# Peer-expert v rows: both halves of a row multiplied in turn, and its ring place released with them

## The reference, cut to what matters

```python
def peer(x, w_q, sub_keys, u_tab, v_tab):
    ...
    best, pos = lax.top_k(cand, PEER_TOPK)
    idx = jnp.take_along_axis(cand_idx, pos, axis=-1).reshape(t, PEER_HEADS * PEER_TOPK)
    gate = jax.nn.softmax(best, axis=-1).reshape(t, PEER_HEADS * PEER_TOPK)
    ...
        act = jax.nn.gelu(jnp.einsum('ted,td->te', jnp.take(u_tab, ib, axis=0), xb).astype(f32),
                          approximate=False)
        w = (gb * act).astype(x.dtype)
        return jnp.einsum('te,ted->td', w, jnp.take(v_tab, ib, axis=0))
```

## Time and profile before

| | |
|---|---|
| median of 3 runs | 3233.33 us (3222.72 to 3244.48) |
| span of the profiled execution | 3176.3 us |
| that execution's own time | not given; the median lies 57.0 us above the span |
| mean granted clock of TensorE | 0.81 of full speed |
| busy: TensorE matmul, VectorE, GpSimd, ScalarE | 63%, 56%, 47%, 12% |
| moved by the gathers (GpSimd's queue) | 805 MB of 959 MB |

### The profile page before, as it was taken

One profiled execution on the slowest core, in us unless ns is written; L12 is line 12 of the kernel. 1 busy time (PEld: TensorE's weight loads), 2 busy tenths in 40 slices (PEclk: granted clock), 3 DMA queues, 4 the chain that ended last, 5 costly groups with the idle time before them and its releaser, 6 DMA issues.

```text
span 3176.3 us, 27801 instructions
## 1 busy us (share of the span) xinstructions
PE 2008.3 (63%) x10194; PEld 1164.2 (37%) x10194; DVE 1763.4 (56%) x3957; ACT 378.2 (12%) x814; POOL 1480.1 (47%) x1540
## 2 busy tenths in 40 slices
PE   5979386668887414438878776677897000067777
PEld 3858275564732413402341165563751000011111
DVE  1622699872286899950070079984176999910000
ACT  1322121112201100000110021112210000000000
POOL 0000144324156565666526634324137777766664
PEclk7979697869998756679989978777999555589999
DMA  6557487547589999999969978656579999999998
GB/s 242 204 197 294 154 338 295 185 150 278 179 288 365 412 385 341 361 379 371 371 229 368 362 279 325 200 171 225 179 252 330 401 410 409 406 364 365 357 352 309
DMA packets 249063, 959.26 MB, mean 302 GB/s; under 512 B 32352, under 2 KB 33504, under 8 KB 231136
## 3 DMA queue, kind: packets, MB, share of 16 engines
q0 software_dynamic: 221184, 805.40, 68.0%
q1 hardware_dynamic: 19584, 142.62, 12.1%
q10 hardware_dynamic: 8160, 9.46, 0.9%
HBM read 955.01 MB, written 2.36 MB: 301 GB/s over the span
## 4 chain that ended last, share of the span: by engine, by line
DVE 26%; DMA 26%; PE 25%; POOL 13%; issue 7%; ACT 2%; ACTq 1%; POOLq 0%; DVEq 0%
PE pb L524 17%; DMA sb_ring<-in_peer_v,sb_idxT 16%; DVE sb_ring L1838 13%; POOL sb_ring L501 13%; DMA sb_ring<-in_peer_u,sb_idxu 8%; PE pv L524 7%; DVE sb_big L1402 1%; PE pb L527 1%; DVE sb_big L1531 1%; DVE sb_big L1550 1%; DVE sb_dec L1492 1%; ACT sb_hT L1017 1%; ACT sb_big L1017 1%; DMA sb_dec<-in_x_prompt 1%; DVE sb_big L1548 1%
## 5 line engine op out<-in xcount | busy, mean ns | idle before, releaser
L501 POOL DMA_INDIRECT sb_ring<-in_peer_u,sb_idxu x768 | 727.9, 948 | 965.4 <-DVE sb_dots L1838 460.9
L501 POOL DMA_INDIRECT sb_ring<-in_peer_v,sb_idxT x768 | 752.0, 979 | 710.0 <-PE pv L524 477.1
L524 PE MATMUL pv<-sb_ring,sb_wcol 128*32 128x512 f32 x3072 | 816.2, 638 | 212.1 <-DMA sb_ring<-in_peer_v,sb_idxT 203.8
L1838 DVE CUSTOM_DVE_ANT_0 sb_ring<-sb_ring,pv 128x1024 f32<-128x1024 f32 x768 | 904.2, 1217 | 27.6 <-DMA sb_ring<-in_peer_u,sb_idxu 14.5
L524 PEld LDWEIGHTS pv<-sb_ring,sb_wcol 128*32 128x32 f32 x3072 | 145.5, 112 | 848.5 <-DMA sb_ring<-in_peer_v,sb_idxT 655.5
L524 PE MATMUL pb<-sb_hT,sb_wring 128*128 128x256 f32 (+1 forms) x1888 | 366.9, 357 | 32.4 <-DMA sb_wring<-in_w_in_blocks 12.7
L524 PEld LDWEIGHTS pb<-sb_hT,sb_wring 128*128 128x128 f32 x1888 | 323.5, 206 | 78.5 <-issue 16.3
L524 PE MATMUL pb<-sb_big 128*128 128x128 f32 (+2 forms) x1888 | 266.5, 315 | 112.9 <-DVE sb_big L1531 82.1
L524 PEld LDWEIGHTS pb<-sb_big 128*128 128x128 f32 (+1 forms) x1888 | 259.7, 225 | 125.1 <-DVE sb_big L1531 87.0
L527 PE MATMUL pb<-sb_cst,sb_dots 128*128 128x128 f32 x6 | 2.7, 451 | 402.1 <-DVE sb_dots L1844 402.1
L1851 DVE COPY sb_accv<-pv 128x1024 f32<-128x1024 f32 x6 | 7.3, 1224 | 392.6 <-PE pv L524 392.5
(11 more groups left out here) (220 smaller groups left out, 1868.0 us busy)
## 6 DMA issues: line engine op xcount, KB each, us to landing
sb_wring<-in_w_in_blocks SPq DMA_DIRECT2D x32, 1024.0 KB, 8.0
sb_ring<-in_w_mod_blocks SPq DMA_DIRECT2D x30, 1024.0 KB, 5.2
sb_wring<-in_w_q_blocks SPq DMA_DIRECT2D x27, 1024.0 KB, 4.9
sb_wring<-in_w_mod_blocks SPq DMA_DIRECT2D x18, 1024.0 KB, 5.0
sb_wring<-in_w_out_blocks SPq DMA_DIRECT2D x13, 1024.0 KB, 7.9
sb_ring<-in_peer_u,sb_idxu POOLq DMA_INDIRECT x768, 7.3
sb_ring<-in_peer_v,sb_idxT POOLq DMA_INDIRECT x768, 6.1
sb_ring<-in_w_in_blocks SPq DMA_DIRECT2D x8, 1024.0 KB, 5.3
```

The lines of the kernel that those rows point to most:

```text
L501: pool.indirect_dma_start(ring[:, j, :], None, a["tab_" + kind][l_of(q)], bass.IndirectOffsetOnAxis(ap=of, axis=0)).then_inc(rows_in[j], 16)
L524: return nc.tensor.matmul(out, lhsT, rhs, start=start, stop=stop)
L1838: dve.tensor_tensor_reduce(out=ring[:, j, :], in0=ring[:, j, :], in1=pv[:, :, :].rearrange("p a b -> p (a b)"), scale=1.0, scalar=0.0, op0 ...
```

## The change

The two loops are exchanged. Row gr waits for its landing, both its halves are multiplied, one after the other in the same strip, and its place is signalled behind the second. No call, operand, wait or signal is added or removed.

```diff
-                        for k in range(2):
-                            for gr in range(GROUPS):
-                                j = h * HB + gr
-                                if k == 0:
-                                    pe.wait_ge(rows_in[j], 16 * (n + i + 1))
-                                o = j * LANES + LANES - 1 - m
+                        for gr in range(GROUPS):
+                            j = h * HB + gr
+                            pe.wait_ge(rows_in[j], 16 * (n + i + 1))
+                            o = j * LANES + LANES - 1 - m
+                            for k in range(2):
                                 last = mm(pv[gr * LANES:gr * LANES + LANES, k, :], wcol[:, i % WCOLS, o:o + LANES],
                                           ring[:, j, k * 512:k * 512 + 512], start=m == 0, stop=m == LANES - 1)
-                                if k:
-                                    last.then_inc(rows_used[j], 1)
+                            last.then_inc(rows_used[j], 1)
```

## The result

The changed kernel took 3256.2 us (median of 14 runs, 3239.9 to 3263.4), the kernel before beside it 3233.0 (14 runs): ratio 1.0068, 95% interval [1.0052, 1.0083]. That is slower by a little, within 1%, where 3157 was forecast.

What follows compares the result with a forecast made beforehand. The v gathers were taken to be bound by a loop of latencies, 11.21 us per 8 rows, with ring places freed only behind the fourth landing. Gains of 84 less 8 given back make 76: 3233.3 - 76 = 3157 us, range 3126 to 3200.

Steps and rivals of the forecast that it cites:

- step (3): New pace of v rows, set by the DMA queue: 1.31 us a row, between 1.28 and 1.36.
- step (4): Gain by stretches: tail 36 us, mixed stages 14, 14, 14 and 6, sum 84.
- Step (2): Loop of one ring place in v items: 8.3 to 8.5 us for 8 rows, so it stops binding.
- Step (1): A v row's four instructions in one strip take 1.90 us; POOL starts 2.16 us after the landing.
- Step (5): Mixed stages: delayed weight blocks give back 8 us, bounds 0 and 20; zero for PE's landing waits and ACT's copies.
- Step (6): On TensorE, another strip's matmuls start while an earlier strip's are pending, against the skill's strict order; the sum relies on it.
- (B): Rival: the DMA queue already bounds the v gathers at 1.41 us; within 1%, 3230 us, chance 0.10.
- (A): Rival: PE runs strips in turn, landed halves cost 3.9 us more; 55 us slower, 3288, chance 0.08.
- (C): Rival: half the gain, v pace 1.36 and nothing from the mixed stages; 41 us less, 3192, chance 0.14.

Runs made afterwards that it cites:

- e14: Changed kernel, unaltered, against the kernel before on a quick chip: ratio 0.975, 3088.5 us.
- e1: New order only in the last two v items, half steps in the gaps keep the old; against the kernel before, quick chip: ratio 0.9879, 39 us less.
- e2: New order only in the half steps in the gaps, last two v items keep the old; against the kernel before, quick chip: ratio 0.9829, 54 us less.
- e8: e1 again, against the kernel before on a slow chip: ratio 1.0009.
- e9: e2 again, against the kernel before on a slow chip: ratio 1.0064.
- e5: Changed kernel, unaltered, against the kernel before on a slow chip: ratio 1.0070, 3257.2 us against 3233.8.
- e6: Kernel before, unaltered, against itself on a slow chip: ratio 1.000.
- e15: e11's kernel against the kernel before on a quick chip: ratio 0.9759, 3092.4 us.
- e11: New order everywhere but in the two attention stages, against the kernel before on a slow chip: ratio 1.0009.
- e12: New order in the two attention stages alone, against the kernel before on a slow chip: ratio 1.0112.

## Why the prediction was wrong

**What failed is step (3), the new pace of 1.31, and with it every term of step (4).** It took the u item's 1.302 as the bound of the next resource for all executions. That is right on quick chips: 1.293 to 1.338 in e14. In the changed kernel's profile, whose 3240.0 us is one of the timed runs, u itself took 1.41 and 1.42, and v came out at 1.434 and 1.484, as before. In place of the queue's rate the loop of one ring place still binds there, through a signal that is 3.5 us late.

**The warning stood in the sum's last line.** "The median of the runs, 3233.3, is 57.0 above the span, for what lies around it. I leave that as it is." One sentence earlier it said that the execution's own time wasn't given. An unexplained 57 us, 1.8% of the span, was named overhead without a row for it. It was 1.8 us of overhead, and the 55 that are left are about what the runs show between a quick and a slow chip (3167 to 3172 against 3217 to 3234), whose limits the profile couldn't show.

**Step (2)** was right on quick chips. In e14 the loop of a ring place no longer binds: the gathers land after 7.7 and 8.0 us, so more are in flight (7.5 to 8 was forecast), at 400 GB/s in the first item (395 to 405). On slow chips the loop still binds: 8.1 us from the issue to the end of the row's matmuls (median of the first v item) and a signal of 3.5 together are 11.6 us, and 11.6/8 = 1.45 for the 1.43 measured. The term mis-sized is the signal: 0.26 from the earlier trace rows, where it is 3.5. Step (1) was too high, without harm: in e14 a row's four instructions take 1.48 us, not 1.90, and follow so closely that the single groups of x4 didn't come.

**Step (4)** on quick chips: the tail was to give 36 us, and e1 gave 39; the mixed stages 48 - 8 = 40, and e2 gave 54. The sum of 76 compares with 79 in e14 (3167.3 - 3088.5). That it comes so near is in part luck, since the two parts measured alone add up to 93. On slow chips e8 and e9 are 2 and 23 us slower than before.

**Step (5)**, bounds 0 and 20 given back for later weight blocks, put zero on TensorE's waits and on ACT's copies: "Zero for both". The stage's own handover from TensorE to ACT had no term at all. Here is the other miss. On slow chips it comes late, and the two attention stages of e5 are 19.9 us longer than those of e6 (142.5 against 122.6, counted as for e9), of 21.2 us between their spans; what the other stretches lose and gain cancels. On quick chips the two stages got shorter, 112.4 in e14 against 120.4 in before, but not by the order in them: in e15, which keeps the old order there, they are 4.5 us shorter still.

**Step (6)** was right against the strict order in Part 3 of the Trainium skill's "TensorE: Matmul & The Clock Gate": the strips start together in the new order too.

**The rivals.** (B), nothing gained, with 0.10, is nearest: it gave 3230 for the timed runs' 3256. Its place was right (no pace gained in the v items) and its mechanism in doubt: it had the queue as the bound, while packets of 159 ns instead of 162, a loop that closes at 11.6 us and the late signals speak for a latency. The busy share of 0.98 that it rested on can't tell: it is 0.98 or 0.99 at 364 GB/s as at 373. What none of the rivals had is the loss of 23 us. (A) and (C) didn't occur.

## What to carry to other kernels

Before a forecast is put on top of a median, the profile's execution must be shown to be one of those timed: where its span is off by more than is accounted for (1.8% here), its rates may be those of another chip, and the rate that is to become the new bound must be priced at both. A release that comes earlier, one row at a time in place of four together, was worth only what the signals delivered, and in a stage shared with other work it can delay that work's own handovers. Where such a stage is short, keep its old order, as e11's kernel does, and take the gain where the gathers run alone.

## What was not expected of the hardware

Chips differ. The tail's u rows took 1.28 to 1.30 us on four and 1.38 to 1.42 on two, and the whole kernel before took 1.4 to 2.1% more on the two. What makes them differ, the chip itself or what surrounds it, isn't shown. The GB/s over 40 slices of a u item show the kind of it, before and then after:

```profile
GB/s 410 410 410 409 411 410 407 405 408 409 408 411 407 410 410 410 410 410 410 410 410 410 410 410 410 410 410 410 410 410 410 408 409 408 405 363 382 419 409 402
```
```profile
GB/s 297 397 412 401 347 380 277 326 402 414 413 405 411 410 410 312 317 389 380 351 384 392 370 328 381 364 387 375 404 354 340 399 376 346 388 342 389 365 376 399
```

The peaks are alike, up to 419 and 414; a slow chip falls to 277 in between. The Trainium skill, "DMA: Bandwidth & Descriptors", Specifications, gives about 358 GB/s as a core's limit from HBM; its section on bandwidth calls this the share when both cores of a pair stream. With one core at work the trace passes it: one chip held 405 to 411 for nearly a whole item, and a slow one reached 414 in slices.

From the release of a ring place to POOL's start it took 0.27 to 0.28 us on the quick chips (median of each item of the tail). On the slow chips it took 2.5 to 5 us in the u items and in the v items of the new order, with TensorE's handovers to ACT late as well. There the trace names "remote" in place of the releaser. Two handovers in such a backlog came 1.42 us apart in e12 (ACT's copies at 774.15 and 775.57), about the time of one row. That they queue behind the gathers' own signals would fit, and is not shown.
